# The first norm of a transformer block: row sums of squares read from x by token rows instead of column sums gathered by GpSimd

## The chip, the cores and the metric

The kernel runs on one core of a Trainium2 chip, in one launch. The metric is the device time in microseconds (us) of that core, from the start of the launch to its end; lower is better. The engines are TensorE (PE in the profile, with its weight loads as PEld), VectorE (DVE), ScalarE (ACT), GpSimd (POOL) and SyncE (SP), which here only issues DMAs.

## What is computed

A block of 1024 tokens by 1024 channels: a norm, one projection that feeds three mixers (a state space mixer, a dilated attention and a forgetting attention), an output projection, and a gated feed-forward part. Only the first norm and the projection behind it matter here:

```python
def rms_norm(x, g):
    xf = x.astype(jnp.float32)
    y = xf * lax.rsqrt(jnp.mean(xf * xf, axis=-1, keepdims=True) + RMS_EPS)
    return (y * g.astype(jnp.float32)).astype(x.dtype)
...
        h = rms_norm(x, g_pre_mix[l])
        proj = h @ w_in[l]
        u_ssm, qkv_dsa, qkv_fox, f_logit = jnp.split(proj, offsets, axis=-1)
```

The root of the norm is one number for each token. The kernel multiplies x, scaled by the gain alone, with the weights, and scales the products by that number afterwards; so the products can start before the root is known, but nothing that leaves PSUM can be used without it. It is needed in three forms: by token rows, one number for each partition (`rn[:, 0, 0:8]`, for the values and the forget gates), by token rows in another order (`rn[:, 0, 8:16]`, for the input of the state space mixer), and as one row of 1024 numbers that is the same on all partitions (`rb`, for q and k).

## The kernel before

Every product of two fp32 matrices is made of three matmuls: each operand is split into a high part, a copy rounded to fp32r that ACT makes, and a low part, the rest, that DVE makes (`op_hi` and `op_lo` of x, `uh` and `ul` of the weights of u, `vh` and `vl` of the weights of the values). All engines run programs of their own that are written out by hand and are joined by semaphores only. What an engine does, it does in the order in which it is written.

The beginning of the kernel runs so:

- SP loads x by channels (`xt`, eight tiles of 128 channels by 1024 tokens, 512 KB each), between them the weights of u (`u_raw`), then the parameters and the first third of the weights of the values (`w_raw`, filled from `w_v`, 1024 KB; the code calls that view of it `v_raw`).
- For each of the eight tiles k, ACT makes `op_hi` (L811), for each second one `uh` (L815), then the squares of the tile (L819, `sq1`, two buffers). DVE makes `op_lo` (L1247) and `ul`. GpSimd adds the squares of the tiles together (helper at L1698, `acc1`, seven adds of 128x1024). ACT waits for GpSimd's adds before it fills a buffer of squares again (`sq_added`).
- PE multiplies tile by tile: 12 matmuls of 512 columns for each k (L1924 to L1926), into four banks. This is called the u stage below. Tile k waits for `x_split` and `uf_split`, that is, for DVE.
- Then the v stage: for each third w of the value weights and each block m of 128 tokens, 24 matmuls of 256 columns (262 for w = 0, L1970 to L1972). It waits for `v_split` (DVE's `vl`), and from the fifth block on for ACT, which has to copy block m - 4 out of its bank (`v_scaled`, L868), scaled by the root.
- Between the blocks of w = 0 stand, in PE's order: behind m = 0 `token_sums` (L1946 and L1948: 16 products of `acc1` with a column of ones give the sums by token rows, in both orders), behind m = 1 `u_transposed` (L1936: 16 transposes of u, which ACT has copied to `ud` with L846), behind m = 3 `norm_sums` (L495: two products of `ones` with `acc1` give the sums as a row on all partitions).
- From each of the two kinds of sums DVE and ACT make the root: `rsqrt_in` (DVE), Ln and Exp (ACT, L509 and L511, behind the load of their function table at L506), `rsqrt_out` (four operations of DVE). For the row form each of these is 128x1024.
- DVE also computes, in the gaps, the small tables of the state space mixer (`coefficient`, `input_matrix`, `abar_powers`, `chunk_rotations`); the last sets the semaphore `powers`, with which GpSimd goes on.

`xr`, spoken of below, is a buffer much later in the kernel, which is loaded from the same tensor `x_tok` (x by token rows) that the change reads.

## Time and profile before

| | us |
|---|---|
| median of 3 runs | 1329.44 |
| lowest and highest | 1327.73, 1332.64 |
| the profiled execution | 1338.54 |
| its span, first to last instruction | 1336.8 |
| PE busy in the span | 1249.6 (93%) |
| DVE, ACT, POOL busy | 763.6, 493.8, 423.9 |
| TensorE's granted clock, mean | 0.97 |

The profiled execution is 9.1 us longer than the median; 1.7 us of it lie outside its span. All positions below are us from the start of the span. PE is busy nearly always, so what shortens or lengthens PE's program, its waits included, moves the end of the kernel. An engine's idle time next to a busy PE costs nothing. A granted clock of 1.00 is TensorE's higher level, 2.4 GHz, and 0.50 the lower one, 1.2 GHz; a value between them is a mean over a stretch that has both.

### The profile page before, as it was taken

What the parts mean: (1) busy time and instruction counts of PE and PEld (TensorE: products, weight loads), DVE (VectorE), ACT (ScalarE), POOL (GpSimd) and SP (SyncE); (2) the same over time, 40 slices, a digit from 0 to 9 for tenths busy, and PEclk for the clock granted to TensorE, in tenths of its full rate; (3) what the DMA queues carried; (4) which work ended last, traced back from release to release, by engine and by line L of the source; (5) the groups of instructions that cost most, each with busy time, mean ns of one, the idle gap of its engine ahead of it and who ended that gap; (6) DMA issues with size and microseconds to landing.
All of it is one profiled execution on the core that took longest, in us unless ns stands there. A gap on an engine that the chain in (4) does not pass through costs nothing.

```text
span 1336.8 us, 18600 instructions
## 1 busy us (share of the span) xinstructions
PE 1249.6 (93%) x6492; PEld 1057.7 (79%) x6492; DVE 763.6 (57%) x1363; ACT 493.8 (37%) x946; POOL 423.9 (32%) x353
## 2 busy tenths in 40 slices
PE   6999999998999997999669999999999989999996
PEld 4899878877888885888558888888888867888885
DVE  7561635247777776675756556556655553333257
ACT  7323112146777773343413333333333332202212
POOL 5049522132555530000922333233323233112200
PEclk8899979998999998999979999999999998999998
DMA  5123243257555521134021222122212146320302
GB/s 197 63 65 94 105 104 141 91 150 207 143 142 141 110 56 63 48 95 142 17 79 48 95 94 82 59 94 94 90 52 94 67 185 252 127 91 36 126 24 103
DMA packets 45782, 135.86 MB, mean 102 GB/s; under 512 B 17126, under 2 KB 17174, under 8 KB 43020
## 3 DMA queue, kind: packets, MB, share of 16 engines
q1 hardware_dynamic: 40140, 117.37, 24.8%
q0 software_dynamic: 5296, 16.87, 6.6%
q10 hardware_dynamic: 288, 0.85, 0.2%
q8 instruction: 36, 0.59, 0.2%
q14 instruction: 22, 0.18, 0.0%
HBM read 98.81 MB, written 35.68 MB: 101 GB/s over the span
## 4 chain that ended last, share of the span: by engine, by line
PE 84%; DVE 8%; issue 3%; ACT 3%; DMA 1%; DVEq 0%; POOL 0%; ACTq 0%; SPq 0%; POOLq 0%
PE ps L2249 18%; PE ps L2228 10%; PE ps L2230 10%; PE ps L2229 10%; PE ps L2176 7%; PE ps L2087 3%; PE ps L488 3%; PE ps L489 3%; PE ps L490 3%; PE ps L2071 2%; PE ps L1970 2%; PE ps L1971 2%; PE ps L1972 2%; PE ps L2072 2%; DVE t_raw L1138 1%
## 5 line engine op out<-in xcount | busy, mean ns | idle before, releaser
L1138 DVE TENSOR_TENSOR ev<-ps,ev 128x512 f32<-128x512 f32 x140 | 94.9, 690 | 120.9 <-PE ps L2230 120.9
L2230 PE MATMUL ps<-t_hi,s_lo 128*128 128x512 f32 x320 | 124.5, 389 | 0.0
L2229 PE MATMUL ps<-t_lo,s_hi 128*128 128x512 f32 x320 | 124.5, 389 | 0.0
L2228 PE MATMUL ps<-t_hi,s_hi 128*128 128x512 f32 x320 | 124.5, 389 | 0.0
L1138 DVE TENSOR_TENSOR z<-ps,z 128x512 f32<-128x512 f32 x80 | 51.5, 686 | 123.2 <-PE ps L2249 122.7
L2228 PE MATMUL ps<-op_hi,s_hi 128*128 128x512 f32 x240 | 94.5, 394 | 10.3 <-DVE s_lo L1138 10.3
L1064 ACT ACTIVATE s_hi<-s_sum 128x512 fp32r<-128x512 f32 x76 | 48.1, 633 | 138.2 <-PE ps L2230 138.2
L1138 DVE TENSOR_TENSOR ptl<-ps,pth 128x512 fp32r<-128x512 f32 (+1 forms) x120 | 76.2, 636 | 32.0 <-ACT pth L954 30.2
L2229 PE MATMUL ps<-ol,s_hi 128*128 128x512 f32 x240 | 94.3, 393 | 0.0
L2230 PE MATMUL ps<-op_hi,s_lo 128*128 128x512 f32 x240 | 94.1, 392 | 0.0
L944 ACT ACTIVATE pr<-ps,nm 128x896 f32<-128x896 f32 (+3 forms) x96 | 71.2, 742 | 31.7 <-DVE nm L1409 30.6
L2087 PE MATMUL ps<-ident,pr 128*128 128x128 f32 x432 | 69.3, 279 | 11.4 <-ACT pr L944 11.4
L1698 POOL TENSOR_TENSOR s_sum<-raw_b 128x512 f32<-128x512 f32 x20 | 33.8, 1692 | 139.0 <-DVE s_lo L1138 139.0
L488 PE MATMUL ps<-op_hi,w_hi 128*128 128x512 f32 x192 | 75.2, 392 | 1.1 <-issue 1.1
L489 PE MATMUL ps<-op_lo,w_hi 128*128 128x512 f32 x192 | 74.7, 389 | 0.0
L490 PE MATMUL ps<-op_hi,w_lo 128*128 128x512 f32 x192 | 74.7, 389 | 0.0
L954 ACT ACTIVATE pth<-ps 128x512 fp32r<-128x512 f32 (+1 forms) x120 | 66.2, 552 | 22.7 <-PE ps L2087 21.7
L2106 PE MATMUL ps<-pth,vs 128*128 128x256 f32 x240 | 69.4, 311 | 0.9 <-DVE ya L1138 0.9
L2229 PEld LDWEIGHTS ps<-t_lo,s_hi 128*128 128x128 f32 x320 | 60.1, 188 | 12.6
L2228 PEld LDWEIGHTS ps<-t_hi,s_hi 128*128 128x128 f32 x320 | 60.1, 188 | 12.5
L2230 PEld LDWEIGHTS ps<-t_hi,s_lo 128*128 128x128 f32 x320 | 60.1, 188 | 12.5
L2249 PE MATMUL ps<-db_hi,hb_hi 128*128 128x512 f32 x192 | 60.4, 396 | 4.1 <-DVE hb_lo L1138 4.1
(331 smaller groups left out, 3262.8 us busy)
## 6 DMA issues: line engine op xcount, KB each, us to landing
hid_scratch<-hf SPq DMA_DIRECT2D x22, 512.0 KB, 2.9
raw_b<-w_stream SPq DMA_DIRECT2D x20, 512.0 KB, 4.8
w_raw<-w_stream SPq DMA_DIRECT2D x16, 512.0 KB, 4.0
qk_scratch<-qk_hi SPq DMA_DIRECT2D x12, 512.0 KB, 2.6
qk_scratch<-qk_lo SPq DMA_DIRECT2D x12, 512.0 KB, 2.9
qa<-qk_scratch POOLq DMA_DIRECT2D x24, 256.0 KB, 4.2
ks<-qk_scratch POOLq DMA_DIRECT2D x24, 256.0 KB, 5.5
hb_raw<-hid_scratch SPq DMA_DIRECT2D x3, 2048.0 KB, 7.2
```

The lines of the kernel that those rows point to most:

```text
L488: e.matmul(out, w_hi[:, j, k, :], x_hi[:, k, half(h)], start=k == 0, stop=False)
L489: e.matmul(out, w_hi[:, j, k, :], x_lo[:, k, half(h)], start=False, stop=False)
L490: last = e.matmul(out, w_lo[:, j, k, :], x_hi[:, k, half(h)], start=False, stop=k == nk - 1)
L944: act.activation(probs(g, r), score_banks(r)[:, 0:width(g, r)], ACT.Exp, scale=-1.0, bias=nm[:, g, r:r + 1], accum_out=den[:, g, r:r + 1]) ...
L1138: return dve.tensor_tensor(out, a, b, op)
L2087: last = pe.transpose(ps[:, 4 + slot % 2, n * P:(n + 1) * P], probs(g, r)[:, (2 * b + a) * P:(2 * b + a + 1) * P], ident[:])
L2106: pe.matmul(out, vs[:, j, 2 * b + a, :], pth[:, slot % 4, cols], start=b == 0 and a == 0, stop=False)
L2176: last = pe.matmul(ps[:, 2 * (m % 2) + n, :], x[:, k, tok(m)], w[:, k, half(n)], start=first, stop=final)
L2228: pe.matmul(out, s_hi[:, j, k], x_hi[:, k, :], start=k == 0, stop=False)
L2229: pe.matmul(out, s_hi[:, j, k], x_lo[:, k, :], start=False, stop=False)
L2230: last = pe.matmul(out, s_lo[:, j, k], x_hi[:, k, :], start=False, stop=k == 3)
L2249: last = pe.matmul(ps[:, 4 + 2 * (m % 2) + b, :], x[:, k, tok(m)], w[:, k, half(b)], start=first, stop=final)
```

## The change

The squares of `xt`, GpSimd's seven adds, `token_sums` and `norm_sums` go. Instead x is read a second time, now by token rows: eight tiles `xq` of 128 tokens by 1024 channels, 512 KB each, in four buffers, issued by SP right behind the first third of the value weights. The last four wait until the squares of the first four are done. ACT squares each tile and lets the instruction sum along the row (`accum_out`), so a tile gives 128 of the sums. Root and Newton step follow on a 128x8 tile. The two other forms of the root come from DRAM: SP writes the 1024 numbers to `r_dram`, waits until they are there, and reads them back in the second order (32 bytes for each partition) and as a row for all partitions (4 KB each).

In PE's program the three waits on the norm go with its matmuls. ACT's squares, the two Sin and the root now stand between `v_high(0)` and the copies of u to `ud`. On DVE `reduced_angle` moves from behind tile 2 to behind tile 3, and `coefficient` from behind tile 7 to behind the root.

```diff
-            sums_bank = ps[:, 7, HALF - 2 * NT:HALF]
...
+                if w == 0:
+                    for m in range(NT):
+                        if m >= 4:
+                            sync.wait_ge(n1s_norm.sums, m - 3)
+                        sync.dma_start(xq[:, m % 4, :], x_tok[:, m, :]).then_inc(xq_in[m % 4], 16)
+                if w == 1:
+                    sync.wait_ge(n1s_norm.rstd, 1)
+                    sync.dma_start(r_dram.rearrange("(m p) -> p m", p=P), rn[:, 0, 0:NT],
+                                   allow_slow_non_contiguous=True).then_inc(r_out, 16)
+                    sync.wait_ge(r_out, 16)
+                    sync.dma_start(rn[:, 0, NT:2 * NT], r_dram.rearrange("(c t) -> c t", t=TS)).then_inc(r_in, 16)
+                    sync.dma_start(rb[:], r_dram.partition_broadcast(P)).then_inc(r_in, 16)
...
-                if k >= 2:
-
-                    act.wait_ge(sq_added, max(1, k - 2))
-                act.activation(sq1[:, k % 2, :], xt[:, k, :], ACT.Square).then_inc(sq_x, 1)
...
-                if k == 4:
-                    act.wait_ge(par_dve, 2)
-                    act.activation(q(SN), q(RR), ACT.Sin)
-                    act.activation(q(SH), q(RR), ACT.Sin, scale=0.5).then_inc(par_act, 1)
...
             v_high(0)
+            for m in range(NT):
+                act.wait_ge(xq_in[m % 4], 16 * (m // 4 + 1))
+                act.activation(xq[:, m % 4, :], xq[:, m % 4, :], ACT.Square,
+                               accum_out=rn[:, 3, m:m + 1]).then_inc(n1s_norm.sums, 1)
+            act.wait_ge(par_dve, 2)
+            act.activation(q(SN), q(RR), ACT.Sin)
+            act.activation(q(SH), q(RR), ACT.Sin, scale=0.5).then_inc(par_act, 1)
+            rsqrt_act(act, n1s_norm, rn[:, 0, 0:NT], rn[:, 1, 0:NT])
 
             act.wait_ge(uf_mm, 1)
-            act.wait_ge(sq_added, KT - 1)
             for k in range(SSM_W // P):
                 for h in range(2):
                     act.activation(ud[:, k, half(h)], ps[:, 2 * k + h, :], ACT.Copy).then_inc(uf_copied, 1)
-            rsqrt_act(act, n1s_norm, rn[:, 0, :], rn[:, 1, :])
...
-                    if w == 0 and m == 4:
-                        rsqrt_act(act, n1_norm, rb[:], n1[:, 0, :])
...
-            between = {1: decay_and_angle, 2: reduced_angle, 7: coefficient}
+            between = {1: decay_and_angle, 3: reduced_angle}
...
             v_low(0)
+            dve.wait_ge(n1s_norm.sums, NT)
+            rsqrt_in(dve, n1s_norm, rn[:, 1, 0:NT], rn[:, 3, 0:NT], D)
+            rsqrt_out(dve, link, n1s_norm, rn[:, 0, 0:NT], rn[:, 1, 0:NT], rn[:, 2, 0:NT])
+            coefficient()
             input_matrix()
-
-            dve.wait_ge(n1s_norm.sums, 1)
-            rsqrt_in(dve, n1s_norm, rn[:, 1, :], sums_bank, D)
-            rsqrt_out(dve, link, n1s_norm, rn[:, 0, :], rn[:, 1, :], rn[:, 2, :])
             v_low(1)
             abar_powers()
-            dve.wait_ge(n1_norm.sums, 2)
-            rsqrt_in(dve, n1_norm, n1[:, 0, :], ps[:, 0:2, :].rearrange("p b n -> p (b n)"), D)
-            rsqrt_out(dve, link, n1_norm, rb[:], n1[:, 0, :], n1[:, 1, :])
             chunk_rotations()
             v_low(2)
-            dve.wait_ge(n1s_norm.rstd, 1)
+            dve.wait_ge(r_in, 32)
...
-            pool.wait_ge(sq_x, 2)
-            tt(acc1[:], sq1[:, 0, :], sq1[:, 1, :], ALU.add).then_inc(sq_added, 1)
-            for k in range(2, KT):
-                pool.wait_ge(sq_x, k + 1)
-                pool.wait_ge(sq_added, k - 1)
-                tt(acc1[:], acc1[:], sq1[:, k % 2, :], ALU.add).then_inc(sq_added, 1)
...
-                    if w == 0 and m == 1:
-                        token_sums()
                     if w == 0 and m == 2:
                         u_transposed()
-                    if w == 0 and m == 3:
-                        pe.wait_ge(n1s_norm.mean, 1)
-                    if w == 0 and m == 4:
-                        pe.wait_ge(uf_copied, 2 * SSM_W // P + TS // 2)
-                        for h in range(2):
-                            norm_sums(pe, n1_norm, acc1, 0, h)
```

Two places in the order of the instructions. The first is ScalarE between the first third of the value weights (`vh`) and the transposed u (`ug`). `ud` is the copy of u that PE transposes, `rn` holds the roots, `sp` the parameters of the state space mixer. Before:

```order
L836 ACTIVATE vh<-w_raw 128x8x256 [waits v_in]
L846 ACTIVATE ud<-ps 128x512 [waits sq_added,uf_mm]
L846 ACTIVATE ud<-ps 128x512 x3
L506 ACT_TABLE_LOAD
L509 ACTIVATE rn<-rn 128x16 [waits n1s_mean]
L511 ACTIVATE rn<-rn 128x16 [waits ln_done]
L850 ACTIVATE ug<-ps 128x2x16x16 [waits ud_mm] x4
```

After:

```order
L841 ACTIVATE xq,rn<-xq 128x1024 [waits xq_in2]
L841 ACTIVATE xq,rn<-xq 128x1024 [waits xq_in3]
L844 ACT_TABLE_LOAD
L844 ACTIVATE sp<-sp 128x8 [waits par_dve]
L845 ACTIVATE sp<-sp 128x8
L500 ACT_TABLE_LOAD
L503 ACTIVATE rn<-rn 128x8 [waits n1s_mean]
L505 ACTIVATE rn<-rn 128x8 [waits ln_done]
L851 ACTIVATE ud<-ps 128x512 [waits uf_mm]
L851 ACTIVATE ud<-ps 128x512 x3
L854 ACTIVATE ug<-ps 128x2x16x16 [waits ud_mm] x4
```

The copies of u, which stood ahead of the root, now stand behind eight squares (the last two are shown), two table loads and the root.

The second is SyncE's queue behind the first third of the value weights, as one piece of the difference. `xq` is x by token rows, `r_scratch` the roots in DRAM:

```order
-L561 DMA w_raw<-w_v 128x2048
-L561 DMA w_raw<-w_v 128x2048 [waits v_split] x2
...
+L555 DMA w_raw<-w_v 128x2048
+L560 DMA xq<-x_tok 128x1024 x4
+L560 DMA xq<-x_tok 128x1024 [waits n1s_sums] x4
+L555 DMA w_raw<-w_v 128x2048 [waits v_split]
+L563 DMA r_scratch<-rn 128x8x1 [waits n1s_rstd]
+L566 DMA rn<-r_scratch 128x8 [waits r_out]
+L567 DMA rb<-r_scratch 128x1024
+L555 DMA w_raw<-w_v 128x2048 [waits v_split]
```

The second and the last third of the value weights moved behind the eight tiles of x and, the last third, behind the way of the roots through DRAM.

## Rows read from the trace of the kernel before

**Rows 1.** The page: span, and the chain that ended last by engine.

```profile
span 1336.8 us, 18600 instructions
...
PE 84%; DVE 8%; issue 3%; ACT 3%; DMA 1%; DVEq 0%; POOL 0%; ACTq 0%; SPq 0%; POOLq 0%
```

**Rows 2.** Stretches: start:end, length, busy (count) of each engine, PEclk, DMA share, GB/s.

```profile
0.00:40.00 40.00, 26.51 (x90) 20.50 (x91) 31.28 (x40) 23.62 (x30) 21.28 (x20) 0.91 0.46 165
40.00:80.00 40.00, 39.34 (x276) 37.76 (x276) 20.76 (x86) 17.47 (x32) 0.00 (x0) 0.91 0.16 54
```

**Rows 3.** Timeline, VectorE: start, us, line, operation, tiles, count, [idle before].

```profile
6.81 1.29 DVE L1247 SCALAR_TENSOR_TENSOR op_lo<-xt,g_sb,op_hi 128x1024 fp32r<-128x1024 f32 x1 [5.68 <-ACT op_hi L811]
...
26.14 6.76 DVE L1247 SCALAR_TENSOR_TENSOR op_lo<-xt,g_sb,op_hi 128x1024 fp32r<-128x1024 f32 x2
```

**Rows 4.** Timeline, GpSimd: the last three adds of squares.

```profile
25.64 9.50 POOL L1698 TENSOR_TENSOR acc<-acc,sq 128x1024 f32<-128x1024 f32 x3 [3.04 <-ACT sq L819]
```

**Rows 5.** Timeline, TensorE in the u stage and at the start of the v stage.

```profile
14.68 0.39 PE L1926 MATMUL ps<-op_hi,ul 128*128 128x512 f32 x1
...
18.00 0.47 PE L1924 MATMUL ps<-op_hi,uh 128*128 128x512 f32 x1 [2.94 <-DVE ul L1138]
...
24.48 0.50 PE L1924 MATMUL ps<-op_hi,uh 128*128 128x512 f32 x1 [1.90 <-DVE op_lo L1247]
...
35.84 0.47 PE L1924 MATMUL ps<-op_hi,uh 128*128 128x512 f32 x1 [1.29 <-DVE ul L1138]
...
42.22 0.39 PE L1970 MATMUL ps<-vh,op_hi 128*128 128x262 f32 x1 [0.66 <-DVE vl L1138]
```

**Rows 6.** Stretches of the u stage, columns as in the second group.

```profile
10.00:20.00 10.00, 7.06 (x25) 5.36 (x24) 9.84 (x6) 8.98 (x14) 7.56 (x3) 0.92 1.03 406
18.00:22.00 4.00, 4.00 (x11) 3.13 (x12) 3.93 (x3) 2.73 (x3) 3.86 (x2) 0.57 0.70 279
24.00:30.00 6.00, 5.52 (x17) 4.41 (x18) 6.00 (x5) 6.00 (x8) 4.21 (x2) 0.72 0.00 0
36.00:41.00 5.00, 5.00 (x23) 4.10 (x23) 4.56 (x20) 0.00 (x0) 0.00 (x0) 1.00 0.02 3
```

**Rows 7.** Timeline, TensorE in the v stage, w = 0.

```profile
45.25 1.84 PE L1946 MATMUL ps<-ones,acc 128*128 128x1 f32 x16
...
50.75 0.56 PE L1970 MATMUL ps<-vh,op_hi 128*128 128x262 f32 x1
...
56.09 1.95 PE L1936 MATMUL ps<-ident,ud 128*128 128x128 f32 x16
57.79 0.37 PE L1970 MATMUL ps<-vh,op_hi 128*128 128x262 f32 x1
...
63.70 1.88 PE L495 MATMUL ps<-acc,ones 128*128 128x512 f32 x4
...
65.54 0.28 PE L1971 MATMUL ps<-vl,op_hi 128*128 128x262 f32 x1
```

**Rows 8.** DMAs to landing: value weights (the first is the longest), `xr` tiles.

```profile
DMA to landing us min/median/max: 4.8/8.6/12.4
...
DMA to landing us min/median/max: 3.7/4.2/4.9
```

**Rows 9.** Timeline, ScalarE: square, split, copies of u, table load, accumulator read.

```profile
10.00 1.04 ACT L819 ACTIVATE sq<-xt 128x1024 f32<-128x1024 f32 x1
...
30.10 1.90 ACT L836 ACTIVATE vh<-w_raw 128x2048 fp32r<-128x2048 f32 x1
...
41.60 2.07 ACT L846 ACTIVATE ud<-ps 128x512 f32<-128x512 f32 x4 [9.60 <-PE ps L1926]
43.68 1.28 ACT L506 ACT_TABLE_LOAD   x1
...
1300.02 0.19 ACT L1122 ACTIVATION_READ_ACCUMULATOR bc<-z 128x1 f32 x1
```

**Rows 10.** DMA issues: 1024 runs of 256 bytes each, median us to landing last.

```profile
v_scratch<-vst SPq DMA_DIRECT2D x12, 256.0 KB, 4.3
```

**Rows 11.** Timeline, SyncE and ScalarE: issue of value weights; the second third's split.

```profile
9.76 53.52 SPq L561 DMA_DIRECT2D w_raw<-w_v  x3
...
77.82 1.92 ACT L836 ACTIVATE vh<-w_raw 128x2048 fp32r<-128x2048 f32 x1
```

More of the change, by code:

```diff
@@ L117, in block_kernel @@
         hid_dram = nc.dram_tensor("hid_scratch", (P, FT, SEQ), f32, kind="Internal").ap()
+        r_dram = nc.dram_tensor("r_scratch", (SEQ,), f32, kind="Internal").ap()
         x2_dram = nc.dram_tensor("x2_scratch", (P, NT, D), f32, kind="Internal").ap()
@@ L141, in block_kernel @@
         ud_mm = sem("ud_mm")
-        x_high, x_split, sq_x, sq_added, uf_high, uf_split, uf_mm, uf_copied, uf_scaled = (sem(n) for n in (
-            "x_high", "x_split", "sq_x", "sq_added", "uf_high", "uf_split", "uf_mm", "uf_copied", "uf_scaled"))
+        xq_in, r_out, r_in = sem_list("xq_in", 4), sem("r_out"), sem("r_in")
+        x_high, x_split, uf_high, uf_split, uf_mm, uf_copied, uf_scaled = (sem(n) for n in (
+            "x_high", "x_split", "uf_high", "uf_split", "uf_mm", "uf_copied", "uf_scaled"))
         v_in, v_high_done, v_split, v_mm, v_scaled, v_out = (sem(n) for n in (
@@ L186, in block_kernel @@
         x2_again = sem_list("x2_again", 2)
-        n1s_norm, n1_norm, nm_norm = (NormSemaphores(sem, n) for n in ("n1s", "n1", "nm"))
+        n1s_norm, nm_norm = (NormSemaphores(sem, n) for n in ("n1s", "nm"))
         zo_norm, h2_norm, ze_norm = (TileNormSemaphores(sem, n) for n in ("zo", "h2", "ze"))
@@ L241, in block_kernel @@
                     [("uh", [P, KT, SSM_W], f32r), ("ul", [P, KT, SSM_W], f32r), ("u_raw", [P, KT, SSM_W], f32),
-                     ("acc1", [P, SEQ], f32), ("vh", [P, 2, KT, VF], f32r), ("vl", [P, 2, KT, VF], f32r)],
+                     ("skip_acc", [P, SEQ], f32), ("vh", [P, 2, KT, VF], f32r), ("vl", [P, 2, KT, VF], f32r)],
                     [("dre", [P, NJ, TS + 1, CH], f32), ("dim", [P, NJ, TS + 1, CH], f32),
@@ L261, in block_kernel @@
         hb_raw, db_raw = r2["hb_raw"], r2["db_raw"]
-        uh, ul, vh, vl, u_raw, acc1 = (r2[n] for n in ("uh", "ul", "vh", "vl", "u_raw", "acc1"))
+        uh, ul, vh, vl, u_raw = (r2[n] for n in ("uh", "ul", "vh", "vl", "u_raw"))
         dre, dim_, ere, eim, ut, tz, mt, mb, pt, wg, row = (r2[n] for n in
@@ L292, in block_kernel @@
                      ("ug", [P, G, TS, CH], f32), ("fl", [P, NT, NH], f32)],
-                    [("sq1", [P, 2, SEQ], f32), ("n1", [P, 2, SEQ], f32)],
+                    [("xq", [P, 4, D], f32)],
                     [("ud", [P, SSM_W // P, SEQ], f32)],
@@ L299, in block_kernel @@
                     [("x2r", [P, NT, D], f32)])
-        w_hi, w_lo, w_raw, ug, fl, sq1, ud, n1, wo_lo, wo_raw, s_hi, s_lo, s_tmp, raw_a, x2r = (r4[n] for n in (
-            "w_hi", "w_lo", "w_raw", "ug", "fl", "sq1", "ud", "n1", "wo_lo", "wo_raw", "s_hi", "s_lo", "s_tmp", "raw_a", "x2r"))
+        w_hi, w_lo, w_raw, ug, fl, xq, ud, wo_lo, wo_raw, s_hi, s_lo, s_tmp, raw_a, x2r = (r4[n] for n in (
+            "w_hi", "w_lo", "w_raw", "ug", "fl", "xq", "ud", "wo_lo", "wo_raw", "s_hi", "s_lo", "s_tmp", "raw_a", "x2r"))
         r5 = region("row_region", 4 * KB, [("rb", [P, SEQ], f32)], [("post_row", [P, D], f32)],
@@ L491, in chunk_products @@
                 last.then_inc(mm_done, 1)
-        def norm_sums(e, norm, acc, bank, h):
-            e.matmul(ps[:, bank + h, :], ones[:], acc[:, half(h)], start=True,
-                     stop=True).then_inc(norm.sums, 1)
         logs = [0]
@@ L1713, in _ @@
                                pattern=[[-1, P]], channel_multiplier=1).then_inc(ident_set, 1)
-            pool.wait_ge(sq_x, 2)
-            tt(acc1[:], sq1[:, 0, :], sq1[:, 1, :], ALU.add).then_inc(sq_added, 1)
-            for k in range(2, KT):
-                pool.wait_ge(sq_x, k + 1)
-                pool.wait_ge(sq_added, k - 1)
-                tt(acc1[:], acc1[:], sq1[:, k % 2, :], ALU.add).then_inc(sq_added, 1)
             pool.wait_ge(uf_mm, 1)
-            pool.wait_ge(n1_norm.sums, 2)
             pool.wait_ge(powers, 1)
@@ L1938, in u_transposed @@
                         last.then_inc(ud_mm, 1)
-            def token_sums():
-                pe.wait_ge(sq_added, KT - 1)
-                pe.wait_ge(ones_set, 1)
-                acc1_c = acc1[:].rearrange("p (c t) -> p t c", t=TS)
-                for m in range(NT):
-                    pe.matmul(sums_bank[:, m:m + 1], acc1[:, m * P:(m + 1) * P], ones[:, 0:1], start=True, stop=True)
-                for t in range(TS):
-                    last = pe.matmul(sums_bank[:, NT + t:NT + t + 1], acc1_c[:, t, :], ones[:, 0:1], start=True, stop=True)
-                last.then_inc(n1s_norm.sums, 1)
             for w in range(NV):
@@ L1976, in _ @@
             pe.wait_ge(uf_scaled, 1)
-            pe.wait_ge(n1s_norm.mean, 1)
             pe.wait_ge(v_scaled, NT)
@@ L1988, in _ @@
                 last.then_inc(s5_pe, 1)
-            pe.wait_ge(n1_norm.mean, 1)
             pe.wait_ge(f_abs, 1)
```

1 line of the change is left out of this document (removed).

## The prediction, made before the changed kernel ran

> **What bounds the kernel now.** I read the page first: PE carries 84% of the chain that ended last [rows 1]. So the question is what the change does to PE's program and to PE's waits. The table of stretches of 40 us shows where PE is not full: 13.5 us idle in the first 40, under 1 us in the next, and in both a mean clock of 0.91 instead of 1.00 [rows 2]. Both lie in the part that the change touches. I then read the timelines of PE, DVE, GpSimd and ACT there. PE waits 2.94, 1.90, 1.29 and 0.66 us, each time for a low part from DVE [rows 5]. DVE is late because of GpSimd: `op_lo` takes 1.29 us alone, but two of them take 6.76 us from 26.14 on [rows 3], just when GpSimd adds squares, 9.50 us for three [rows 4]. Behind 42 us PE has no wait in this part, but it does work for the norm.
>
> **The u stage.** Removed: ACT's eight squares, GpSimd's seven adds. That GpSimd's adds are what stretches DVE is read from their overlap, and I take it that DVE goes back to 1.2 us for `op_lo` and 0.7 us or less for `ul`. Its work for a tile is then 1.2 + 0.35 = 1.6 us; PE's is 12 matmuls of 0.227 us (22 in 5.0 us at clock 1.00 [rows 6]), that is 2.73 us. PE is the slower one, and from tile 2 on nothing should stop it. Tile 1 ends with the matmul that starts at 14.68 [rows 5], so at 14.91. Tile 2 needs x loaded by about 11 us, which it was (DMA moved 406 GB/s between 10 and 20 us [rows 6]); its splits are done at about 13.9. The last tile of x is loaded at about 18.7 (my estimate, from the bytes queued ahead of it at that rate and some 1.3 us to land), DVE is through with it at 22, PE wants it at 28.5. Both clock dips in this stage (0.57 over 4 us, 0.72 over 6 us: 1.7 us lost each [rows 6]) followed waits that are gone. So PE ends the u stage at 14.91 + 6 x 2.73 = 31.3. `vl`, the next thing needed, is ready at 22.2 + 1.9 + 2.3 = 26.4: the first value weights land at 9.76 + 12.4 = 22.2 [rows 8, 11], ACT's split takes 1.90 [rows 9], and DVE's as much and a bit. The v stage starts at 31.3 instead of 42.22 [rows 5]: **gain 10.9 us**.
>
> **`token_sums` and what follows it.** Before, from 42.22 to the first matmul of block m = 2 at 57.79 it is 15.6 us: block 0 in 3.0, the sums in 5.5 (45.25 to 50.75), block 1 in 5.3 (50.75 to 56.09), transposes in 1.7 [rows 7]. Blocks 2 and 3 take 5.9 together (57.79 to 63.70), so 2.95 is the full-clock price and block 1 paid 2.4 more at the low clock behind the tiny matmuls. Without them the stretch is 2 x 2.95 + 1.7 = 7.6 us. **Gain 8.0 us**, if PE need not wait for the transposes' input.
>
> **The new wait.** It does have to. The transposes need `ud`, and ACT's copies to `ud` now stand behind the squares of `xq`, the Sin pair and the root. ACT's chain: its split of value weights ends at 24.1. The queue is then still full; at 406 GB/s a tile of 524 KB takes 1.3 us, so the first four tiles of `xq` are there at 23.5 to 27.4. A square is 1.04 us and reading the sum adds at most 0.19 [rows 9]; I take 1.1. The fifth tile is issued when the first square is done, at 25.2, and needs the 4.2 us that the same tensor's tiles need later [rows 8]: 29.4; the other three follow at the queue's pace, to 33.2. All squares are done at 34.3. Then two table loads of 1.28 [rows 9], the Sin pair and Ln and Exp with 0.3 us each: 37.5. DVE's part of the root hides behind the table loads. The four copies take 2.07 [rows 9]: 39.6. PE comes to the transposes at 31.3 + 5.9 = 37.2. **Wait 2.4 us.** Its bounds: squares back to back from 24.1 would end at 32.5, a wait of 0.6; landings of 4.9 us and some more queueing would make it 4. The wait may pull the clock down: the waits of 2.94 and 1.90 were each followed by a dip of 1.7 us, that of 1.29 was not [rows 5, 6]. I charge 1.2 us, since the transposes take 1.7 us of the slow stretch and took the same at either level. Bounds 0 and 1.7. **Loss 3.6 us.**
>
> The Trainium skill ("DMA: Bandwidth & Descriptors", Where 436 GB/s comes from) says that for a transfer from HBM to SBUF the HBM side binds, at about 358 GB/s for a core. The trace has 406 over ten microseconds at this very place [rows 6], so the measurement decides; by the page a tile would take 1.46 us instead of 1.3, the last one would land some 0.6 us later, and the sum would be 0.6 us smaller.
>
> **`norm_sums`.** 63.70 to 65.42 (the regular pace resumes with the matmul at 65.54 [rows 7]): **gain 1.7 us**.
>
> **Edits at nothing.** The row form of the root (five DVE operations and two of ACT, 128x1024) stood beside a full PE and goes without a gain. `coefficient`, moved behind the root, is needed by DVE's own later tables, which end earlier than before; GpSimd, waiting for `powers` until 86 us, starts about 25 us earlier. The second third of the value weights is issued at about 28.5, behind the tiles of `xq`, and lands by 36; ACT wants it at 41.6. `ug`'s scaling and the first use of `rb` come more than 20 us after the roots are back from DRAM. SP waits for that write with the last third of the weights queued behind; the price of this is in the last rival.
>
> **Sum.** 10.9 + 8.0 - 3.6 + 1.7 = 17.0 us. All behind it waits for PE or is waited for by PE at the same distance, so the gain should reach the end whole. The profiled execution would go from 1338.54 to 1321.5. I take the same difference off the median: 1329.44 - 17.0 = **1312.4 us**.
>
> **Rivals.**
>
> *No wait at the transposes.* The squares run at ACT's pace and the first loads come sooner. Gain 10.9 + 8.0 + 1.7 = 20.6, time 1308.8. For it: only 2.4 us are missing. Against it: even the lower bound leaves 0.6.
>
> *The loads of `xq` do not overlap.* If each of the last four took its 4.2 us by itself, from 25.2 on, the squares would end at 43.1, ACT would be ready at 48.4 and PE would wait 11.2 instead of 2.4: gain 8.2, time 1321.2. Against it: eight tiles of `xt` in one queue ran at 406 GB/s. For it: each of these four waits for a square, so the queue can run dry.
>
> *DVE stays slow.* If something else than the adds stretched DVE, the v stage would start at 42.2 as before; ACT would be ready, and the gain would be 8.0 + 1.7 = 9.7, time 1319.7. For it: the dips of DVE come only here, next to other traffic (all loads of x). Against it: the 6.76 us lie at 26 to 33, where DMA moved nothing [rows 6].
>
> *Slower: the way through DRAM.* The write of the roots is 1024 pieces of 4 bytes, at about 38 us, and SP can't issue the last third of the value weights until it has landed. PE needs that third at about 83 (its split, at 77.82 before [rows 11], moves with PE, and the load, the split and the low part take 4.8, 1.9 and 2.3 [rows 8, 9]), so it must be issued by 74. From 36 us for the write on, each more costs one. To lose over 6.6 us against before (0.5%), it would have to take 60. The nearest row is 1024 pieces of 256 bytes in 4.3 us [rows 10], an upper bound unless tiny writes cost more than large ones.
>
> The Trainium skill ("DMA: Bandwidth & Descriptors", Rules for kernel authors) warns of this: a strided last dimension becomes one descriptor for each element, and should be rearranged. No row here has 4-byte pieces; the rule gives no time, so it only makes the count of 1024 the right one.
>
> *The gain is given back later.* A later DMA or ACT stage that is not PE's could become late. It would have to eat over 10 us to leave less than 0.5%; I see no such wait.
>
> **Chances and range.** Forecast 0.55; no wait 0.12; loads don't overlap 0.12; DVE stays slow 0.08; given back 0.08; slower 0.05. The range goes from 1307 (no wait, and 2 us for the spread of the runs) to 1321 (the two slower gains). A change of 0.5%, 6.6 us, is about what the measurement tells from none: the first four cases make 0.87, and some of the fifth still leaves over 0.5%; faster by more 0.90, within 0.06, slower by more 0.04.
>
> **What would show it.** Right: `op_lo` at 1.3 us throughout, no wait of PE in the u stage behind tile 1, the v stage at 31 to 32 us, one wait of PE of 1 to 4 us just before the transposes, released by ACT's copies of u, and the split of the last third of the value weights about 17 us earlier than 77.82 [rows 11]. Wrong: PE waits in the u stage, ACT waiting for `xq` more than 5 us in all, or a wait for the last third of the value weights.

## The result, and the profile after

The changed kernel takes 1317.55 us (median of four runs, 1315.35 to 1319.53) where the kernel before, run beside it, takes 1329.91 (four runs, 1327.73 to 1332.64): a ratio of 0.988, 95% interval 0.985 to 0.991. Two further comparisons on other chips gave 0.988 [0.985, 0.991] each. So it is faster by 1.2%, some 16 us by the ratio (12 to 21 by its interval). The medians themselves lie 12.4 us apart here, and 17.3 and 14.4 in the two other comparisons. 17.0 us were forecast; 1312.4 was 5 us too low for this median, and the range 1307 to 1321 holds it. The profiled execution of after took 1319.53 us, that of before 1338.54.

The page of the kernel after, answering to [rows 1]: span, and the chain that ended last.

```profile
span 1317.4 us, 18522 instructions
...
PE 85%; DVE 5%; issue 3%; ACT 3%; DMA 2%; SPq 1%; DVEq 0%; POOL 0%; ACTq 0%
```

The stretches of after that answer to [rows 2, 6]: start:end, length, busy (count) of PE, PEld, DVE, ACT, POOL, then PEclk, DMA share, GB/s.

```profile
0.00:40.00 40.00, 30.25 (x144) 25.67 (x144) 17.06 (x30) 28.39 (x44) 2.04 (x13) 1.00 0.82 296
40.00:80.00 40.00, 39.02 (x303) 39.05 (x304) 24.55 (x131) 14.05 (x29) 14.81 (x24) 0.92 0.35 93
```

```profile
40.00:44.00 4.00, 3.02 (x14) 3.04 (x15) 3.50 (x21) 2.22 (x5) 0.00 (x0) 0.50 0.12 1
44.00:48.00 4.00, 4.00 (x24) 4.00 (x24) 1.49 (x4) 3.74 (x7) 0.00 (x0) 0.65 0.01 2
```

The clock of the first 40 us went from 0.91 to 1.00 and PE's busy time from 26.5 to 30.3 us. The one gap behind the start is at 37.8 to 41.0 us, and with it comes the one clock dip of these 80 us: 0.50, TensorE's lower level of 1.2 GHz, over the whole of 40 to 44 us, and part of 44 to 48. Before the gap PE had worked without a stop since 7.6 us, and since 12.8 us at the pace of the full clock, a matmul of 512 columns each 0.23 us. Up to there it is 0.43 us, in before too, which the mean clock of 1.00 does not show.

VectorE's timeline of after, answering to [rows 3]:

```profile
18.15 2.47 DVE L1248 SCALAR_TENSOR_TENSOR op_lo<-xt,g_sb,op_hi 128x1024 fp32r<-128x1024 f32 x2
20.54 0.68 DVE L1139 TENSOR_TENSOR ul<-u_raw,uh 128x512 fp32r<-128x512 f32 x1
21.14 1.28 DVE L1248 SCALAR_TENSOR_TENSOR op_lo<-xt,g_sb,op_hi 128x1024 fp32r<-128x1024 f32 x1
```

Two `op_lo` take 2.47 us here, where they took 6.76. DVE is through with the last tile at 22.4 instead of 36.9. TensorE's timeline of after, answering to [rows 5, 7]:

```profile
31.83 0.28 PE L1939 MATMUL ps<-vh,op_hi 128*128 128x262 f32 x1
...
40.98 3.65 PE L1925 MATMUL ps<-ident,ud 128*128 128x128 f32 x16 [3.14 <-ACT ud L851]
44.29 0.57 PE L1939 MATMUL ps<-vh,op_hi 128*128 128x262 f32 x1
```

The v stage starts at 31.83 without a wait, 10.4 us earlier than 42.22. The transposes then wait 3.14 us for ACT's copies to `ud`, and 3.31 us pass from their first start to the next block (44.29 - 40.98), where [rows 7] had 1.70 (57.79 - 56.09). ACT's timeline of after shows why the copies are late (left out: the other squares, the reads of the accumulator, 0.18 to 0.19 us each, and the Sin pair, Ln and Exp, some 0.2 us each):

```profile
22.64 1.92 ACT L834 ACTIVATE vh<-w_raw 128x2048 fp32r<-128x2048 f32 x1 [2.03 <-DMA w_raw<-w_v]
24.47 1.04 ACT L841 ACTIVATE xq<-xq 128x1024 f32<-128x1024 f32 x1
...
29.84 1.06 ACT L841 ACTIVATE xq<-xq 128x1024 f32<-128x1024 f32 x1 [1.00 <-DMA xq<-x_tok]
...
31.32 1.06 ACT L841 ACTIVATE xq<-xq 128x1024 f32<-128x1024 f32 x1 [0.33 <-DMA xq<-x_tok]
...
33.15 1.06 ACT L841 ACTIVATE xq<-xq 128x1024 f32<-128x1024 f32 x1 [0.68 <-DMA xq<-x_tok]
...
35.53 1.28 ACT L844 ACT_TABLE_LOAD   x1
...
37.15 1.28 ACT L500 ACT_TABLE_LOAD   x1
...
38.80 2.04 ACT L851 ACTIVATE ud<-ps 128x512 f32<-128x512 f32 x4
```

Three waits for `xq`, 2.0 us in all, then two table loads, 2.56 us, stand ahead of the copies. Last, SyncE's queue of after (answering to [rows 11]) and the landing of the roots' DMA (the column behind KB is us from issue to landing):

```profile
10.47 18.72 SPq L560 DMA_DIRECT2D xq<-x_tok  x8
29.24 0.43 SPq L555 DMA_DIRECT2D w_raw<-w_v  x1
39.73 0.39 SPq L563 DMA_DIRECT2D r_scratch<-rn  x1
48.53 0.33 SPq L566 DMA_DIRECT2D rn<-r_scratch  x1
...
49.79 0.44 SPq L555 DMA_DIRECT2D w_raw<-w_v  x1
```

```profile
r_scratch<-rn SPq DMA_DIRECT2D x1, 4.0 KB, 8.8
```

The roots' 4 KB need 8.8 us to DRAM. Only SP waits for it; it issues the last third of the weights at 49.79, and ACT splits them at 63.77 without a wait, 14.05 us earlier than before (77.82; that row of [rows 11] is the split of the last third and not of the second, which stands at 58.66).

To follow the gain, here are three starts on PE for every kernel below, in us of its profiled execution, and the mean clock from 40 to 50 us. The starts are those of the v stage, of its block m = 2 (the first work behind the transposes), and of the first product of the q/k stage (line 488), which lies behind everything that the change touches.

```
kernel                     v stage   block 2   q/k stage   clock 40:50
before                      42.22     57.79     126.70      0.96
before_again                41.70     57.16     126.38      0.92
after                       31.83     44.29     112.43      0.66
after_again                 30.80     42.12     110.27      0.83
after_third                 31.68     44.16     112.26      0.67
e_no_adds                   31.68     47.60     116.53      0.69
e_no_adds_one_sum           32.10     39.87     108.79      1.00
e_ud_first                  31.71     39.52     107.20      1.00
e_ud_first_again            31.02     38.60     106.26      1.00
e_sin_early                 32.46     40.12     107.11      1.00
e_sin_early_ud_first        31.80     39.37     106.38      1.00
e_both_again                32.21     39.78     106.79      1.00
e_half_loads                32.04     39.61     106.62      1.00
e_six_writes                30.81     43.20     151.60      0.83
```

Between executions of one kernel these starts differ by up to 2.2 us. By the means of the two kernels, the change brings 14.9 us up to the q/k stage (126.54 - 111.65).

### The profile page after: what moved, and what is told of

Read it like the earlier page. It is cut to its first block, busy times and chain, and to the rows that moved or that the text cites. A ratio compares the mean times of both kernels' runs of the same rounds, so it can differ in the third digit from the quotient of the medians.

```text
span 1317.4 us, 18522 instructions
## 1 busy us (share of the span) xinstructions
PE 1232.8 (94%) x6456; PEld 1045.4 (79%) x6456; DVE 745.5 (57%) x1358; ACT 492.5 (37%) x951; POOL 403.4 (31%) x346
## 4 chain that ended last, share of the span: by engine, by line
PE 85%; DVE 5%; issue 3%; ACT 3%; DMA 2%; SPq 1%; DVEq 0%; POOL 0%; ACTq 0%
PE ps L2216 18%; PE ps L2195 10%; PE ps L2196 10%; PE ps L2197 10%; PE ps L2143 7%; PE ps L488 3%; PE ps L490 3%; PE ps L489 3%; PE ps L2054 3%; PE ps L2038 2%; PE ps L1940 2%; PE ps L1939 2%; PE ps L1941 2%; PE ps L2039 1%; DVE t_raw L1139 1%
## 5 line engine op out<-in xcount | busy, mean ns | idle before, releaser
L2195 PEld LDWEIGHTS ps<-t_hi,s_hi 128*128 128x128 f32 x320 | 60.2, 188 | 12.6
L2197 PEld LDWEIGHTS ps<-t_hi,s_lo 128*128 128x128 f32 x320 | 60.1, 188 | 12.6
```

What stands on the lines that cost most here:

```text
L2195: pe.matmul(out, s_hi[:, j, k], x_hi[:, k, :], start=k == 0, stop=False)
L2197: last = pe.matmul(out, s_lo[:, j, k], x_hi[:, k, :], start=False, stop=k == 3)
```

## The experiments

They ran on three chips, and each is compared with the kernel before on its own chip: before_again, after_again, e_no_adds and e_no_adds_one_sum on the first (before there: median 1333.09 us), e_ud_first, e_sin_early_ud_first, e_half_loads and e_six_writes on the second (1332.99), e_sin_early, e_both_again, e_ud_first_again and after_third on the third (1334.12). Behind each time stands the ratio to before with its 95% interval.

**The kernel before, once more** (before_again, no edit).

> The kernel before, unchanged. Time: the same as before, within 3 us. Its profile tells apart two explanations of the 6 us by which the two profiled executions drift apart between 170 and 235 us of the span, in the part with many small matmuls, where the granted clock of before was 0.83 and that of after higher. If the dip is chance of the execution, this profile has a mean clock of 0.9 or more between 160 and 200 us, and a span of 1328 to 1333; if it belongs to the program before, the clock is 0.83 again and the span 1336.

1332.91 us, ratio 1.001 [0.998, 1.004], 10 runs from 1329 to 1342. The width matters: the profiled execution of before had taken 1338.54, this one 1333.85. The stretch 180:190 of the two (columns as above), first of the kernel before as profiled at first, then of before_again:

```profile
180.00:190.00 10.00, 9.32 (x78) 7.85 (x78) 1.22 (x1) 3.07 (x4) 5.25 (x9) 0.54 0.39 40
```

```profile
180.00:190.00 10.00, 9.82 (x91) 8.62 (x92) 7.22 (x6) 2.02 (x3) 6.92 (x9) 1.00 0.82 119
```

The same program ran this piece at clock 0.54 once and at 1.00 the other time, as the first of the two explanations has it: the dip is chance. 10 x (1 - 0.54) = 4.6 us is my estimate of its price. Of the 19.0 us between the profiled executions of before and after, 14.3 lie ahead of the q/k stage (126.70 - 112.43). The other 4.7 go with this dip and not with the change: from the q/k stage to the end of the span it is 1210.1 us in before, but 1205.7 in before_again and 1205.0 in after.

**The kernel after, twice more** (after_again and after_third, no edit).

> The changed kernel, unchanged. Theory: the early part is worth 14.3 us (v stage 31.8 instead of 42.2, 3.1 us of wait for the copies of u, and a clock dip behind it), so the ratio to before is 0.989 and the median 1315 to 1317. Rival (the gain is the 19.4 us between the two profiled spans): 0.985 and 1311.

> The changed kernel, unchanged, for comparison on the same chip. 1315 to 1317, ratio to before 0.986 to 0.990; first qk product between 110 and 112.5.

1315.82 us (ratio 0.988 [0.985, 0.991]) and 1319.71 (0.988 [0.985, 0.991]). The ratios are as forecast, the second median is 2.7 us above its forecast. The wait repeats to a few hundredths; the length of the transposes does not. First after_again, then after_third:

```profile
39.93 2.53 PE L1925 MATMUL ps<-ident,ud 128*128 128x128 f32 x16 [3.13 <-ACT ud L851]
42.12 0.57 PE L1939 MATMUL ps<-vh,op_hi 128*128 128x262 f32 x1
```

```profile
40.86 3.65 PE L1925 MATMUL ps<-ident,ud 128*128 128x128 f32 x16 [3.17 <-ACT ud L851]
44.16 0.57 PE L1939 MATMUL ps<-vh,op_hi 128*128 128x262 f32 x1
```

From the first transpose to the block behind it is 2.19 and 3.30 us: the dip comes each time, and once some of the transposes ran ahead of it.

**Before without GpSimd's adds** (e_no_adds). Is it GpSimd that stretches DVE? The squares of the last tile go straight to `acc1`, so the norm's sums hold the last tile alone; everything else of before stands, ACT's squares too.

```diff
-                    act.wait_ge(sq_added, max(1, k - 2))
-                act.activation(sq1[:, k % 2, :], xt[:, k, :], ACT.Square).then_inc(sq_x, 1)
+                    act.wait_ge(sq_x, k - 1)
+                act.activation(acc1[:] if k == KT - 1 else sq1[:, k % 2, :], xt[:, k, :], ACT.Square).then_inc(sq_x, 1)
...
-            tt(acc1[:], sq1[:, 0, :], sq1[:, 1, :], ALU.add).then_inc(sq_added, 1)
-            for k in range(2, KT):
-                pool.wait_ge(sq_x, k + 1)
-                pool.wait_ge(sq_added, k - 1)
-                tt(acc1[:], acc1[:], sq1[:, k % 2, :], ALU.add).then_inc(sq_added, 1)
```

> Before without GpSimd's seven adds of squares. ACT still makes all eight squares, the last one goes to the accumulator, and the sums are those of the last tile alone; everything else is as before. Theory (the adds stretch VectorE's op_lo and ul): op_lo 1.3 us throughout, no wait of TensorE behind tile 1 of the u stage, v stage from 31.5 us instead of 42.2, kernel 10 to 11 us faster, 1319. Rival (VectorE is slowed by the loads of x or by ScalarE): op_lo up to 3 us as before, v stage from about 40, kernel faster by less than 2 us.

1325.40 us, ratio 0.995 [0.993, 0.997]. Its VectorE:

```profile
20.56 1.28 DVE L1246 SCALAR_TENSOR_TENSOR op_lo<-xt,g_sb,op_hi 128x1024 fp32r<-128x1024 f32 x1 [2.25 <-ACT op_hi L811]
22.55 1.28 DVE L1246 SCALAR_TENSOR_TENSOR op_lo<-xt,g_sb,op_hi 128x1024 fp32r<-128x1024 f32 x1 [0.70 <-ACT op_hi L811]
...
25.05 1.28 DVE L1246 SCALAR_TENSOR_TENSOR op_lo<-xt,g_sb,op_hi 128x1024 fp32r<-128x1024 f32 x1 [0.62 <-ACT op_hi L811]
```

`op_lo` is back at 1.28 us with all loads of x and all of ACT's squares still there: the rival that something else slows DVE falls. DVE now waits for ACT, which still squares, but PE does not notice; the v stage starts at 31.68, as in after. Against before_again that is 10.0 us for the adds alone, and 9.9 are still there at the q/k stage. The median moved less than the 10 to 11 us forecast (7.7 us, by the ratio 6.4, at most 9.3). Its ten runs reach from 1319.30 to 1331.29. The lowest lies 9.9 us under the lowest of before on this chip (1329.22), and its mean clock is 0.982, that of the longest 0.973. So clock dips in later stages are the likely place of the rest, but no run shows which.

How GpSimd does it is to be seen in before_again, the stretch in which it adds tiles 2 to 4. VectorE, then GpSimd, each add in a row of its own:

```profile
14.47 2.85 DVE L1138 TENSOR_TENSOR ul<-u_raw,uh 128x512 fp32r<-128x512 f32 x1
17.24 2.34 DVE L1162 TENSOR_SCALAR sp<-sp 128x8 f32<-128x8 f32 x1
19.62 0.17 DVE L1163 TENSOR_SCALAR sp<-sp 128x8 f32<-128x8 f32 x1
19.83 2.27 DVE L1168 SCALAR_TENSOR_TENSOR sp<-sp 128x8 f32<-128x8 f32 x1
```

```profile
14.31 2.46 POOL L1698 TENSOR_TENSOR acc<-acc,sq 128x1024 f32<-128x1024 f32 x1 [1.18 <-ACT sq L819]
16.91 2.64 POOL L1698 TENSOR_TENSOR acc<-acc,sq 128x1024 f32<-128x1024 f32 x1
19.70 2.38 POOL L1698 TENSOR_TENSOR acc<-acc,sq 128x1024 f32<-128x1024 f32 x1
```

The adds end at 16.77, 19.55 and 22.08. An operation on 8 columns, 0.17 us in after, lasts from 17.24 to 19.58, another, 0.17 us in after as well, from 19.83 to 22.10: each ends when an add ends. DVE isn't slowed in proportion, it is stopped until the add is through. It goes the other way too: in the same trace the two adds that run beside two `op_lo` (3.41 and 3.44 us each instead of 1.28) last 3.22 and 3.19 us, where these three last 2.38 to 2.64. The Trainium skill (SBUF — State Buffer, Who interferes with whom) has the rule: a VectorE instruction with two SBUF inputs contends with a GpSimd instruction that reads SBUF, over a shared pair of ports that is an exclusive lock. The trace agrees for the operation at 19.83, which has two inputs, with 2.27 us for what takes 0.17, and for `op_lo` and `ul`. The one at 17.24 has a single input; for such the page says it only of certain modes, and no run shows in which mode it ran.

**That, and one product for the sixteen** (e_no_adds_one_sum). What do the sixteen one-column products cost? They become one product of 16 columns, which sums the first 128 tokens for all; the adds stay out.

```diff
-                for m in range(NT):
-                    pe.matmul(sums_bank[:, m:m + 1], acc1[:, m * P:(m + 1) * P], ones[:, 0:1], start=True, stop=True)
-                for t in range(TS):
-                    last = pe.matmul(sums_bank[:, NT + t:NT + t + 1], acc1_c[:, t, :], ones[:, 0:1], start=True, stop=True)
+                last = pe.matmul(sums_bank[:], acc1[:, 0:P], ones[:, 0:2 * NT], start=True, stop=True)
```

> As the kernel without GpSimd's adds, and the 16 one-column products for the sums by token rows are one product with 16 columns (which gives one block's sum 16 times, so the sums of the other blocks are left out). Theory: 5.5 us of TensorE go, and the clock dip behind them with 2.4 us: a further 7.5 to 8 us, 1311, with block 1 of w = 0 in 3.0 us instead of 5.3. Rival (the dip comes anyway, later): a further 5.5 us, 1313.5.

1313.48 us, ratio 0.986 [0.983, 0.990]. Its TensorE:

```profile
35.03 0.29 PE L1938 MATMUL ps<-ones,acc 128*128 128x16 f32 x2
35.17 0.37 PE L1960 MATMUL ps<-vh,op_hi 128*128 128x262 f32 x1
...
38.16 1.95 PE L1929 MATMUL ps<-ident,ud 128*128 128x128 f32 x16
```

The sums take 0.14 us instead of 5.5, and block 1 behind them 2.99 instead of 5.3: 7.7 us earlier than e_no_adds at block 2, still 7.7 at the q/k stage. This was the step of 8.0, and the clock dip behind the tiny products went with them, as the theory has it. The median fits the rival's 1313.5, but that is chance: the medians of the two kernels lie 11.9 us apart, 4 more than their starts. Both kernels leave out work that the norm needs, the adds here and there and most of the sums, so they price the parts of the gain; whether a whole kernel could have it without reading x twice, no run shows.

**Copies of u ahead of Sin and root** (e_ud_first and e_ud_first_again). Does the wait at the transposes cost what it seems to? The copies follow the last square at once.

```diff
-            act.wait_ge(par_dve, 2)
-            act.activation(q(SN), q(RR), ACT.Sin)
-            act.activation(q(SH), q(RR), ACT.Sin, scale=0.5).then_inc(par_act, 1)
-            rsqrt_act(act, n1s_norm, rn[:, 0, 0:NT], rn[:, 1, 0:NT])
+            act.wait_ge(n1s_norm.sums, NT)
             act.wait_ge(uf_mm, 1)
             for k in range(SSM_W // P):
                 for h in range(2):
                     act.activation(ud[:, k, half(h)], ps[:, 2 * k + h, :], ACT.Copy).then_inc(uf_copied, 1)
+            act.wait_ge(par_dve, 2)
+            act.activation(q(SN), q(RR), ACT.Sin)
+            act.activation(q(SH), q(RR), ACT.Sin, scale=0.5).then_inc(par_act, 1)
+            rsqrt_act(act, n1s_norm, rn[:, 0, 0:NT], rn[:, 1, 0:NT])
```

> The changed kernel with ScalarE's four copies of u moved ahead of the Sin pair and the root, directly behind the squares. Theory (the transposes wait for these copies, and the clock dips because of that wait): the squares end at 35.4, the copies at 37.6, TensorE comes at 37.7 and does not wait; transposes in 1.7 us instead of 3.3 or 2.2; block 2 at 39.5 instead of 44.3 or 42.1, first qk product at 106 to 107 instead of 112.4 or 110.3; 4 to 6 us faster than the changed kernel, 1310 to 1312. Rival (the root itself is late, block 4 waits for the scaled copy of block 0): the wait moves to block 4 and the gain is under 2 us.

> The kernel with only the copies of u moved, again. Its early part was 5.2 and 3.1 us shorter than in the two profiles of the changed kernel (first qk product at 107.2), yet its median was not lower. Theory (clock dips later in the span, between 160 and 200 us and around 300, 500 and 650 us, hid it): now 1310 to 1314, with the first qk product at 107. Rival (something later takes the gain back): 1315 to 1317 again.

1315.89 us (0.985 [0.983, 0.988]) and 1314.44 (0.986 [0.983, 0.989]). Its TensorE:

```profile
37.73 2.03 PE L1926 MATMUL ps<-ident,ud 128*128 128x128 f32 x16
39.52 0.37 PE L1940 MATMUL ps<-vh,op_hi 128*128 128x262 f32 x1
```

No wait, no dip (clock 1.00 from 40 to 60), the transposes take 1.79 us again. The q/k stage starts at 107.20 and 106.26, some 5 us earlier than in after, as forecast, so the rival falls. The times do not show it as clearly: the first median misses its forecast of 1310 to 1312, the second lies between the theory's range and the rival's. By the ratios it is 3 to 4 us, within their intervals; on the third chip the medians are 5.3 us apart (1319.71 - 1314.44). One later dip can be named: from 156 to 170 us the clock is 0.51 in the first profile and 1.00 in the second.

**The Sin pair ahead of the value weights' split, alone (e_sin_early) and with the copies first (e_sin_early_ud_first and e_both_again).** The second way to shorten ACT's chain: the Sin pair and its table load move into the 2.03 us in which ACT waits for the first value weights.

```diff
+            act.wait_ge(par_dve, 2)
+            act.activation(q(SN), q(RR), ACT.Sin)
+            act.activation(q(SH), q(RR), ACT.Sin, scale=0.5).then_inc(par_act, 1)
             act.wait_ge(bc_in, 16 * 3)
```

> The changed kernel with only the Sin pair and its table load moved into ScalarE's idle gap before the first split of value weights; the copies of u stay behind the root. Theory: the root and the copies come 1.6 us earlier, TensorE waits 1.5 us before the transposes instead of 3.1. A wait of 1.29 us was followed by no clock dip, one of 1.90 by one; so either no dip (first qk product at 107.5 to 108) or one (109 to 110.5). Rival: ScalarE's chain is set by the loads of x, the squares end later, and the wait stays over 2.5 us.

> As the kernel with the copies of u first, and the Sin pair with its table load stands behind the last split of x, where ScalarE sat idle for 2.0 us waiting for the value weights. Theory: the 1.6 us fit into that gap, so the root is ready 1.6 us earlier than with the copies alone; TensorE at most 0.5 us faster than there, 1310. Rival: the table load is late, pushes the squares, and the copies of u come after TensorE: 1 to 2 us slower than with the copies alone.

> The kernel with the Sin pair early and the copies of u ahead of the root, again, beside the changed kernel on the same chip. Theory: no wait before the transposes, first qk product at 106.4 as in its first profile, 4 to 6 us faster than the changed kernel, 1310 to 1312. Rival (its first result was a draw of the clock): within 2 us of the changed kernel.

Sin alone: 1314.28 us, 0.985 [0.982, 0.987]. Both: 1311.82, 0.984 [0.981, 0.986], and again 1311.13, 0.983 [0.981, 0.985]. In the run with Sin alone ACT's wait for the value weights shrinks from 2.03 to 0.38 us, and one table load is left behind the squares:

```profile
19.60 1.28 ACT L837 ACT_TABLE_LOAD   x1
...
21.71 1.93 ACT L834 ACTIVATE vh<-w_raw 128x2048 fp32r<-128x2048 f32 x1 [0.38 <-DMA w_raw<-w_v]
...
34.50 1.28 ACT L500 ACT_TABLE_LOAD   x1
...
36.15 2.04 ACT L851 ACTIVATE ud<-ps 128x512 f32<-128x512 f32 x4
```

The copies end at 38.2, and PE, which comes at 38.33 in this execution, no longer waits, where 1.5 us of wait were forecast. The edit gave 1.6 us; beyond it the squares ended 0.9 us earlier than in after, and PE came 0.5 us later. With the timing of after some 1.4 us of wait would be left (my estimate, 40.84 - 1.6 - 37.84), so this profile does not show that the Sin edit alone is enough. With both edits the version has the lowest median of all whose work is whole: 8.6 us under after_third on the third chip, 6 to 7 us by the ratios to before, whose intervals just touch (0.981 to 0.985 and 0.985 to 0.991). At the q/k stage it is 5.5 us earlier than after_third; the rest of the 8.6 is not in the part that was changed. Against e_ud_first it is no earlier there (106.4 and 106.8 against 107.2 and 106.3). From block 2 to the q/k stage it takes 67.0 us where e_ud_first takes 67.7, since PE waits 0.87 us for DVE's `fz` at that stage and not 1.5; whether 0.7 us is left of this at the end stays open.

**Half the loads of `xq`** (e_half_loads). Is the queue of `xq` the part of the wait that was mis-sized? Only four tiles are loaded and each is squared twice (the second time as it then stands), so the sums are of four tiles; ACT's work is the same.

```diff
-                    for m in range(NT):
-                        if m >= 4:
-                            sync.wait_ge(n1s_norm.sums, m - 3)
+                    for m in range(4):
```

> The changed kernel without the last four tiles of x by token rows: ScalarE squares the first four tiles twice, so the sums of tokens 512 to 1023 are left out (their places hold others). Theory (2.7 us of the chain of squares are waits for loads): squares end at 32.8 instead of 35.4, TensorE's wait before the transposes falls from 3.1 to under 0.6 us, and the clock dip goes with it; first qk product at 107 to 108; 4 to 5 us faster than the changed kernel. Rival (the dip comes from the transposes, not from the wait): 2.7 us faster.

1312.42 us, 0.984 [0.981, 0.987]. The squares end at 32.2 instead of 35.4 (2.5 us of it the waits for loads, 8.5 us from first to last square instead of 10.9; the rest an earlier start), and PE comes to the transposes at 37.89 and finds `ud` ready, since 37.6. At the q/k stage that is 5.0 us under the mean of after (111.65), for 3.1 us of wait: the dip went with the wait, and the rival's 2.7 falls.

**Six writes of the roots** (e_six_writes). Where is the threshold of the way through DRAM? The write is issued six times, each waited for.

```diff
-                    sync.dma_start(r_dram.rearrange("(m p) -> p m", p=P), rn[:, 0, 0:NT],
-                                   allow_slow_non_contiguous=True).then_inc(r_out, 16)
-                    sync.wait_ge(r_out, 16)
+                    for again in range(6):
+                        sync.dma_start(r_dram.rearrange("(m p) -> p m", p=P), rn[:, 0, 0:NT],
+                                       allow_slow_non_contiguous=True).then_inc(r_out, 16)
+                        sync.wait_ge(r_out, 16 * (again + 1))
```

> The changed kernel with the write of the roots to DRAM made six times, each waited for. One write took 8.8 us, so the last ends at about 93 us instead of 48.5, and the last third of the value weights is issued behind it. The prediction has a threshold of 36 us for the write. Theory: TensorE waits for the last third from 86 to about 103, so the kernel is 14 to 20 us slower than the changed one, 1331 to 1337. Rival (the threshold is wrong by far, or repeated writes are faster): under 5 us.

1358.06 us, ratio 1.018 [1.015, 1.022]: slower than before, and some 40 us slower than after, where 14 to 20 were forecast. SyncE, ScalarE and TensorE of that run:

```profile
39.25 51.60 SPq L564 DMA_DIRECT2D r_scratch<-rn  x6
100.50 0.33 SPq L567 DMA_DIRECT2D rn<-r_scratch  x1
...
101.36 0.43 SPq L555 DMA_DIRECT2D w_raw<-w_v  x1
```

```profile
109.06 1.91 ACT L835 ACTIVATE vh<-w_raw 128x2048 fp32r<-128x2048 f32 x1 [46.73 <-DMA w_raw<-w_v]
```

```profile
111.39 0.58 PE L1940 MATMUL ps<-vh,op_hi 128*128 128x256 f32 x1 [38.28 <-ACT vst L870]
```

The writes take 61.2 us, 10.2 each. The wait was to be expected at the start of the third of the value products, w = 2, at about 86 us. It came at 73.1, in w = 1, and PE does not wait for weights but for ACT's evictions (`vst`): the split of the last third stands in ACT's program ahead of the evictions of w = 1, and ACT runs in order. So ACT stands still for 46.73 us, the accumulators fill after four blocks (61.50 to 73.11), and PE stops. The stop alone is 38.3 of the 40 us. From this run the threshold is 61.2 - 38.3 = 22.9 us for the write, not 36.

## Why the prediction was right, and where it was not

By the mean starts of the table (before 41.96, 57.48, 126.54; after 31.44, 43.52, 111.65):

- **The u stage, 10.9: measured 10.5.** The mechanism is shown by e_no_adds: take the adds away and only them, and `op_lo` takes what it takes in after, PE has no wait in the stage, and the v stage starts at 31.68 (after: 31.83). That after reached 31.83 and after_again 30.80, around the 31.3 forecast, comes from the first tiles: PE's matmuls reach the pace of the full clock at 12.6 us in one and at 10.5 in the other.
- **`token_sums`, 8.0: measured 7.9.** Without wait or dip it is 7.6 us from the v stage to block 2 (e_sin_early_ud_first: 39.37 - 31.80), and 15.5 before. e_no_adds_one_sum, which takes only the small products away from e_no_adds, finds 7.7.
- **The wait, 2.4: measured 3.1 to 3.3**, inside its bounds (3.13 to 3.17 in the rows, 3.3 by the starts). ACT's copies were through at 40.8 and not at 39.6, PE came at 37.8 and not at 37.2. The term that was too small is the landing of `xq`: the squares took 10.9 us from 24.5 on, where the sum had 10.2 from 24.1 on. The fifth tile was there at 29.8, nearly as forecast (29.4), but the next two came 1.5 and 1.8 us apart, where the sum had 1.3. While the fifth was under way the queue moved 283 GB/s, not 406:

```profile
24.00:28.00 4.00, 4.00 (x20) 3.30 (x19) 2.41 (x2) 3.99 (x8) 0.00 (x0) 1.00 0.85 283
```

  This is the fear behind the second rival, but it cost 1 us and not 9. Whether the queue was slower because each load waits for a square, no run separates. e_half_loads removes this term alone; its 2.5 us, and an execution in which PE came late, are enough for the wait to go.
- **The clock dip behind it, 1.2: measured 1.6, 2.7 and 2.7, outside its bounds of 0 and 1.7 in two of three. This is the step that failed.** It rested on "the transposes take 1.7 us of the slow stretch and took the same at either level". But the 1.7 us of [rows 7], 56.09 to 57.79, lie behind the dip, not in it. Two stretches of before show it, the one ahead of the transposes and the one with them:

```profile
54.00:56.00 2.00, 2.00 (x11) 2.00 (x11) 0.00 (x0) 0.00 (x0) 0.00 (x0) 0.50 0.00 0
56.00:58.00 2.00, 2.00 (x20) 2.00 (x20) 0.00 (x0) 1.27 (x3) 0.00 (x0) 1.00 0.00 0
```

  At 0.50 they take 3.3 us, as after shows. With 1.1 us that the blocks behind lose (68.1 from block 2 to the q/k stage in after, 67.0 in e_sin_early, e_sin_early_ud_first and e_both_again) the dip costs 2.7 us in after, about what its clock says (3.0 us of work at 0.50 and 4 at 0.65: 1.5 + 1.4). In each of the six profiles of the changed kernel without the wait there is no dip ahead of the q/k stage; in e_six_writes, which has a wait of 3.68 us there, it comes too.
- **`norm_sums`, 1.7: measured 2.1** (69.1 us from block 2 to the q/k stage before, 67.0 without a dip). The rest is not the sums: at the first product of the q/k stage PE sat idle for 1.09 and 1.38 us in the two profiles of before, for 0.87 in after.

10.5 + 7.9 - 3.3 - 2.3 + 2.1 = 14.9 us at the q/k stage, where the forecast had 17.0; the parts are read from the same starts, so their sum must be that of the table. The ratio says 16 with an interval of some 4 us either way, so it can't tell the two, and that 17.0 came so near to 16 is in part luck: 2.1 us too much in the sum. Of the 5.2 us between 1312.4 and 1317.55 these 2.1 are a step of the sum; the other 3 are not, and lie within the spread of single runs.

**Given back later: no.** From the q/k stage to the end of the span the two profiles of before take 1210.1 and 1205.7 us, the three of after 1205.0, 1203.7 and 1205.0. Nothing is lost there that these differences between single executions would let one see.

**The way through DRAM** was harmless as forecast, for weaker reasons than given. "An upper bound unless tiny writes cost more" was the wrong side: 1024 pieces of 4 bytes took 8.8 us where as many of 256 took 4.3 [rows 10]. And the threshold of 36 us overlooked the order of ACT's program. The slack that was left is 14 us (22.9 - 8.8), not the 27 that 36 would leave. The Trainium skill (DMA: Bandwidth & Descriptors, Rules for kernel authors) has the rule that such a transfer becomes one descriptor for each element; the time agrees with it as a price of pieces: the same 4 KB came back, as 128 pieces of 32 bytes, in 3.6 us.

**The Trainium skill's 358 GB/s** would have made the sum smaller by 0.6 us. Between 12 and 20 us after moved 414:

```profile
12.00:20.00 8.00, 8.00 (x35) 6.63 (x34) 7.54 (x13) 6.65 (x10) 0.00 (x0) 1.00 1.05 414
```

So the limit named there does not hold for this core, which runs alone, and the slower landings of the last `xq` tiles are not due to it. Another page of the Trainium skill (Perfetto Trace Analysis, Roofline) says so: 358 is the share when both cores of a pair read, one alone is bound by its 16 DMA engines at about 435. The 414 agree with that.

## What to carry to other kernels

Adds on GpSimd beside VectorE's two-input operations aren't free help (here they cost PE 10 us): look for a VectorE instruction that ends when a GpSimd one does, and price what PE then waits. A wait of PE in a dense stage can cost more than itself: here 3.1 us of wait cost 1.6 to 2.7 more at the lower clock, one of 1.29 us [rows 5] nothing. If you charge such a dip, look for rows that lie in one, by their granted clock, before you say that an instruction takes the same at either level. When you give a transfer its slack, follow the waiting engine's program in order: what stands behind the wait, evictions above all, sets the threshold, not the consumer of the data.
